# Cache pages of the compressed branch: from two DMA queues to three, with half of them on GpSimd's

## The reference, cut to what matters

```python
past_kc = cc_l[page_table, :, 0].reshape(bs, -1, N_KV, HEAD_DIM)
past_vc = cc_l[page_table, :, 1].reshape(bs, -1, N_KV, HEAD_DIM)
...
def compress(x_raw, pe, w):
    B, Tk = x_raw.shape[:2]
    xb = x_raw.reshape(B, Tk // CMP_BLOCK, CMP_BLOCK, N_KV, HEAD_DIM) + pe[:, None, :]
    return jnp.einsum('bnlgd,lde->bnge', xb, w)
...
    k = rmsnorm(compress(kc_raw, pe[0], w[0]), k_norm_c)
    v = compress(vc_raw, pe[1], w[1])
```

## Time and profile before

| what | us |
|---|---|
| median of 3 runs (4289.74 to 4298.05) | 4290.12 |
| the profiled execution, its own time | 4288.17 |
| its span, from the first to the last instruction | 4286.3 |
| TensorE busy with matmuls, whole span | 3773.1 (88%) |
| VectorE, ScalarE, GpSimd busy, whole span | 1556.0, 941.9, 818.9 |
| first matmul on a cache page to the end of the last | 748.35 to 1081.26 |

### The profile page before, as it was taken

One profiled execution on the slowest core, in us unless ns is written; L12 is line 12 of the kernel. 1 busy time (PEld: TensorE's weight loads), 2 busy tenths in 40 slices (PEclk: granted clock), 3 DMA queues, 4 the chain that ended last, 5 costly groups with the idle time before them and its releaser, 6 DMA issues. The chain is left out here.

```text
span 4286.3 us, 64338 instructions
## 1 busy us (share of the span) xinstructions
PE 3773.1 (88%) x23270; PEld 3191.8 (74%) x23270; DVE 1556.0 (36%) x3867; ACT 941.9 (22%) x2029; POOL 818.9 (19%) x969
## 2 busy tenths in 40 slices
PE   8999997534689999996379999999999999999998
PEld 6888885434466776765368888888888888888887
DVE  4344341010666666552013223432234322432223
ACT  1000000000356666653002111221022100221012
POOL 1010100000254323121002122221222211222112
PEclk9999998777799999997569999999999999999999
DMA  4101005666565443222234555645556555555553
GB/s 166 43 13 55 21 15 172 213 191 196 146 165 139 114 114 102 77 65 77 72 129 142 152 151 169 183 140 151 152 163 179 152 151 152 167 155 152 151 152 109
DMA packets 372823, 558.02 MB, mean 130 GB/s; under 512 B 55655, under 2 KB 155808, under 8 KB 371369
## 3 DMA queue, kind: packets, MB, share of 16 engines
q1 hardware_dynamic: 320984, 502.54, 40.5%
q10 hardware_dynamic: 50697, 43.79, 3.4%
q0 software_dynamic: 864, 7.85, 0.5%
HBM read 480.28 MB, written 78.50 MB: 130 GB/s over the span
## 5 line engine op out<-in xcount | busy, mean ns | idle before, releaser
L319 PE MATMUL ps_z<-x_gained,w_in_sb 128*128 128x257 f32 x2816 | 620.5, 380 | 20.6 <-DVE x_gained L355 20.6
L319 PEld LDWEIGHTS ps_z<-x_gained,w_in_sb 128*128 128x128 f32 x2816 | 533.0, 189 | 102.5 <-issue 21.6
L1746 PE MATMUL ps_tx<-ff,w_ring 128*128 128x257 f32 x1280 | 305.1, 380 | 7.8 <-DVE ff L1894 7.8
L980 ACT ACTIVATE PT_pr<-ps_p 128x384 f32<-128x384 f32 (+4 forms) x576 | 256.6, 496 | 243.6 <-PE ps_p L927 219.5
L1746 PE MATMUL ps_ty<-ff_sums,w_ring 128*128 128x257 f32 x1280 | 305.3, 380 | 0.0
L1746 PE MATMUL ps_ty<-h_sums,w_ring 128*128 128x257 f32 x1280 | 304.2, 379 | 0.2 <-issue 0.2
L1746 PE MATMUL ps_tx<-h_gained,w_ring 128*128 128x257 f32 x1280 | 303.3, 379 | 0.0
L1746 PEld LDWEIGHTS ps_tx<-ff,w_ring 128*128 128x128 f32 x1280 | 242.6, 190 | 44.3 <-issue 8.2
L1746 PEld LDWEIGHTS ps_ty<-ff_sums,w_ring 128*128 128x128 f32 x1280 | 243.1, 190 | 36.8
L1746 PEld LDWEIGHTS ps_ty<-h_sums,w_ring 128*128 128x128 f32 x1280 | 242.2, 189 | 36.7 <-issue 0.6
L1856 POOL TENSOR_TENSOR h<-h,u 128x257 f32<-128x257 f32 x192 | 135.4, 705 | 696.2 <-DVE u L1983 305.8
(11 more groups left out here) (291 smaller groups left out, 5442.4 us busy)
## 6 DMA issues: line engine op xcount, KB each, us to landing
w_ring<-scratch_w_sums SPq DMA_DIRECT2D x640, 256.0 KB, 2.6
w_ring<-in_w_tail SPq DMA_DIRECT2D x480, 256.0 KB, 2.6
w_blocks_pr<-in_w_tail SPq DMA_DIRECT2D x40, 1024.0 KB, 8.2
scratch_w_sums<-w_blocks_pr SPq DMA_DIRECT2D x40, 1024.0 KB, 5.4
pages<-in_cache_cmp SPq DMA_DIRECT2D x256, 128.0 KB, 3.5
pages<-in_cache_cmp ACTq DMA_DIRECT2D x256, 128.0 KB, 3.8
w_in_sb<-in_w_in SPq DMA_DIRECT2D x22, 512.0 KB, 13.8
x_chunk<-in_xT SPq DMA_DIRECT2D x16, 514.0 KB, 6.9
```

The lines of the kernel that those rows point to most:

```text
L319: mm = pe.matmul(o, wg[:, k] if name == "g" else win[:, m, k], aT[:, c % 2, k, h * HF:(h + 1) * HF], start=(k == 0), stop=(k == KT - 1))
L980: act.activation(PT[0:rows, turn_no[x] % 3, g, 0:128 * w], tbank(k, g)[0:rows, 0:w], ACT.Copy).then_inc(s_cp, 1)
L1746: mm = pe.matmul(bank[:, 0:HF], w[:, k], b, start=(name in ("P1", "P6", "P5") and k == 0), stop=(name in ("P2", "P4", "P3") and k == 3), s ...
```

## The change

A buffer's 32 pages are divided into three shares: pages 0 to 7 go to SP, 8 to 15 to ScalarE and 16 to 31 to GpSimd. GpSimd's DMAs count on semaphores of their own, `s_pp`, and TensorE waits for both counts. GpSimd loads its pages of the first turn ahead of the three DMAs of the band, and those of the other seven turns behind them.

```diff
+        s_pp = [ctx.enter_context(nc.semaphore(f"cp_software_pages{b}")) for b in range(2)]
...
-        HALF, AT_ONCE = NPG // 2, 8
+        SHARES = ((0, 8, 8), (8, 8, 8), (16, 16, 8))
...
-                with eng.Fori(0, HALF // AT_ONCE) as j:
-                    base = j * AT_ONCE + HALF * side
+                first, n_pages, at_once = SHARES[side]
+                with eng.Fori(0, n_pages // at_once) as j:
+                    base = j * at_once + first
...
-                                      d["cache_cmp"][ds(page, 1)].rearrange("a p k n -> (a p) k n")).then_inc(s_pg[b], 16)
+                                      d["cache_cmp"][ds(page, 1)].rearrange("a p k n -> (a p) k n")).then_inc((s_pp if side == 2 else s_pg)[b], 16)
...
                 pool.dma_start(cmask[:], d["cmask"]).then_inc(s_cm, 16)
+                pool.wait_ge(s_c, ONE + 16)
+                load_pages(pool, 2, 0)
                 pool.wait_ge(s_line, 3)
...
                 pool.dma_start(t["band"][:], src).then_inc(s_band, 16)
+                with pool.Fori(0, NIT - 1) as i:
+                    load_pages(pool, 2, i + 1)
...
-                        pe.wait_ge(s_pg[b], ONE + 16 * NPG * (i + 1))
+                        pe.wait_ge(s_pg[b], ONE + 16 * 16 * (i + 1))
+                        pe.wait_ge(s_pp[b], 16 * 16 * (i + 1))
```

More of the change, by code:

```diff
@@ L480, in load_pages @@
                 plain(eng)
-                with eng.Fori(0, HALF // AT_ONCE) as j:
-                    base = j * AT_ONCE + HALF * side
+                first, n_pages, at_once = SHARES[side]
+                with eng.Fori(0, n_pages // at_once) as j:
+                    base = j * at_once + first
                     pages = [eng.value_load(ptab[0:1, ds(i * (2 * NPG) + (base + (NPG * b + x)), 1)], min_val=0,
-                                            max_val=d["cache_cmp"].shape[0] - 1) for x in range(AT_ONCE)]
+                                            max_val=d["cache_cmp"].shape[0] - 1) for x in range(at_once)]
                     for x, page in enumerate(pages):
                         eng.dma_start(pg[b][:, ds(base + x, 1)].rearrange("p a k n -> p (a k) n"),
-                                      d["cache_cmp"][ds(page, 1)].rearrange("a p k n -> (a p) k n")).then_inc(s_pg[b], 16)
+                                      d["cache_cmp"][ds(page, 1)].rearrange("a p k n -> (a p) k n")).then_inc((s_pp if side == 2 else s_pg)[b], 16)
         with nc.Block() as block:
```

## The result

| kernel | median us | runs |
|---|---|---|
| before | 4287.31 | 7 (4281.52 to 4298.05) |
| changed | 4305.9 | 7 (4304.03 to 4312.24) |

The ratio is 1.0046 with an interval of 1.0033 to 1.0058: the changed kernel is **slower by about 18.6 us**. The profiled execution of the changed kernel took 4312.24 us (span 4310.5), the highest of its seven, so its 24 us over the profiled execution of before are more than the medians differ by. The prediction was 4223 and faster.

The account below looks back on a forecast made before the run. ScalarE's full instruction stream was taken to bound the 44.5 us turn. Loop 208u - 288.4 plus start debt 48u - 44.2 gave -66.4 us at u = 1.04, so 4223 us, range 4200 to 4355.

Parts of the forecast that it names:

- u: What one page costs GpSimd's stream in the cache loop: 1.04 us, giving a turn of 33.3 us.
- the register steps with the hand-over: In GpSimd's page price: steps around an issue 0.18 us, handing the DMA over some 0.03.
- a quarter of the backlog: Part of GpSimd's issue backlog (2.9 us per eight DMAs) not hidden beside the sequencer: 0.08 us a page.
- rival 1: GpSimd's stream becomes longest: 4350 us if its sequencer stands still per issue, 4480 at 16 ns a row; chance 0.21.
- the formula 256u - 332.6: Whole run's change in us, six and a half loop turns plus the late start: -66.4 at u = 1.04.
- The band's chain: GpSimd's three dependent bias-band DMAs, standing behind its first 32 pages: 33.7 us counted before the second turn's pages.
- the landing L: Time for a buffer's pages to land after issue, before its chunk: taken as 7 us, between 3.6 and 9.2.
- The start debt: Delay of buffer 0's second-turn chunk behind GpSimd's first pages and band: 48u - 44.2, 5.7 us.
- rival 3: In the loop, transfers already bind at 190 GB/s, turn stays 44.5 us: 4294 us, no change; chance 0.04.
- Rival 2: GpSimd's issue backlog isn't queued at all, u = 1.33: 4296 us, no change to slightly slower; chance 0.08.
- Rival 4: GpSimd reads the table faster than ScalarE, u = 0.85, turn of 28 us: about 4176 us; chance 0.06.
- The break-even u = 1.30: GpSimd's page price in us at which the summed change is zero; above it the kernel gets slower.

Follow-up runs that it names:

- experiment 1: Changed kernel with GpSimd reading one table entry and issuing that page's DMA at once, instead of eight reads then eight issues: 4311.56 us.
- experiment 6: Changed kernel with GpSimd's loop written out, without table reads or address registers, loading the same 16 pages of each buffer every turn: 4188.27 us, one run.
- experiment 2: Changed kernel with GpSimd's table reads left out, loading pages 16 to 31 of the pool every turn by the same loop: 4185.22 us.
- experiment 3: Changed kernel with the band's three DMAs put between GpSimd's pages of the first two turns, so it waits for none: 4295.98 us.
- experiment 8: Shares 11, 10, 11 and 11, 11, 10 with the band between, each engine's table reads moved ahead of its buffer wait: 4185.62 and 4179.69 us.
- experiment 5: Changed kernel with each GpSimd page loaded as two DMAs of 64 rows instead of one of 128: 4482.99 us, one run.
- experiment 7: Changed kernel, band's DMAs between pages, SP/ScalarE/GpSimd shares 12, 10, 10; 11, 10, 11; 11, 11, 10: 4211.6, 4208.67, 4214.2 us.

## Why the prediction was wrong

**The step that failed is u, GpSimd's price of a page: 1.04 forecast, 1.42 measured.** The terms, one by one: the read 0.69, measured 0.71; the register steps with the hand-over, 0.18 + 0.03, measured 0.10; the loop 0.06, measured 0.07 (1.42 - 0.71 - 0.64); and the DMA itself, put beside the sequencer but for a quarter of the backlog (0.08), measured 0.53 (experiments 1 and 6). The last term is 0.45 too low, and the register steps, 0.11 too high, hide a part of it. (A quarter of the backlog is 0.09, not 0.08; that slip is worth 2.6 us.) The sequencer stands still for each issue, and a read can't begin until it goes on: the mechanism of rival 1, at a price a little under its 1.54, because the steps around an issue were cheaper.

Two rows had led to it. GpSimd's drain that began at 743.6 beside the band's DMA of 743.58 was read as a sequencer that goes on while an issue is handled. By experiment 1 it goes on when the DMA *begins*; a stand ahead of that left no row there, as GpSimd was waiting anyway. And the three constants stood 0.66 and 0.50 us apart with no register step between them. That spacing, 0.58 on average, is near the 0.53 that issues back to back cost in experiment 6; I took it as a sign of a low price.

**The rest of the sum held, with two errors that cancel in part.** With u = 1.42 the formula 256u - 332.6 gives +31; the last chunk came 18.9 later. By its terms:

- The first 32 pages took 742.71 - 699.4 = 43.3 us for 45.4 by the formula: -2.1.
- The band's chain took 24.3 us (742.71 to 766.99) for 33.7: -9.4. It now ran in a stretch where the DMA engines were busy for 0.85 rather than 1.00, with the first line's DMA 4.2 us on its way in place of 11.0. That the load is why was not tried.
- From the band's issue to buffer 0's chunk 23.9 us for 29.7: -5.8, 4.7 of it the landing L. The page that this chunk waited for landed 2.3 us after its DMA began, and not 7.
- Six turns and a half took 300.7 us for 295.4: +5.3, most of it hold-ups of GpSimd's issues, the longest two 1.00 and 2.84 us:

```profile
877.39 4.36 POOL L488 DMA_DIRECT2D pages<-in_cache_cmp  x7 [1.00 <-issue]
...
937.12 4.42 POOL L488 DMA_DIRECT2D pages<-in_cache_cmp  x7 [2.84 <-issue]
```

VectorE masks the band beside the first; beside the second it has no instruction. What held them was not settled. They are 0.7 us of the 1.5 by which the turn of 47.1 exceeds its stream of 45.6. The rest is the landing of a buffer's last page, 2.3 us at buffer 0's chunk of the second turn and 7.0 at that of the eighth. In the loop itself, then, the forecast's L of 7 was about right.

That is 30.9 - 17.3 + 5.3 = 18.9. The start debt was forecast at 5.7 and measured 790.93 - 784.30 = 6.6: near, but by a longer stream and a shorter chain than I had.

**What was right:** the issue set the turn, not the transfers (rival 3 fell in experiment 2); with ScalarE's load halved its square was no longer waited for; SP and ScalarE were off the path in the changed kernel; the band's chain delayed the second turn (experiment 3). Rival 2 had u at 1.33 and no change or slightly slower, near in its time by luck, as the chain and the landing were priced too high. Its sequencer only waits for its backlog; experiment 1 shows it standing ahead of a DMA even with none. Rival 4 fell on its price for a read: 0.71, no cheaper than ScalarE's 0.69. The break-even u = 1.30 agrees with the sign: 1.42 lies above it.

The Trainium skill, page "DMA: Bandwidth & Descriptors", section "Issuing engines are not separate DMA queues", has the sequencer's time as usually small beside the transfer. Here it is not. On SP or ScalarE a page took 1.28 us of the queue's time before, and its 128 KB take 0.44 us at the 296 GB/s that experiment 8 reached with the same bytes; the two queues before moved 190.

## What to carry to other kernels

When work is to be shared out over queues, price an item on each of them by rows of its own, and where there are none, by the spacing of back-to-back issues: an engine that shows idle may have a sequencer that isn't. Give each queue a share by that price, and not by how free its engine looks; half of the pages on GpSimd lost 0.5%, a quarter won 1.6%, and about a third won 1.7 to 2.6% with the band's DMAs between the pages and, at the best, the reads ahead of the wait. Then look for the ring of a buffer: whatever doesn't need the free buffer, such as reading addresses, belongs ahead of the wait for it.

## What the hardware showed that I had not expected

- GpSimd's sequencer is taken for about 0.53 us by each DMA ahead of its start, for 64 rows as for 128, with an idle engine as with a busy one (experiments 1 and 5; the spacing in 6 agrees). The 16 ns a row that the 16.4 us drain allowed don't exist in these transfers: 128 rows would have taken 2.05 us. The length of a drain is no measure of rows either: in the changed kernel it lasts 9.5 us behind a DMA of 128 rows, as its row on L491 says.

```profile
L491 POOLq DRAIN  x1: 9512/9512/9512, 1089.2 to 1089.2; - x1
```

- How soon a page landed went with what else was on its way, more than with who issued it. In the changed kernel GpSimd's median is 2.6 us for 5.1 and 5.3 of SP's and ScalarE's. But most of GpSimd's DMAs go while the other two queues are quiet. The eight that begin from 807.1 to 811.7, beside pages of both others, take 3.6 to 6.6 us (the first line below), and the last pages of most buffers 5 to 7. With 11, 10 and 11 pages (experiment 7) the order of GpSimd and ScalarE is the other way round:

```profile
DMA to landing us min/median/max: 3.6/6.0/6.6
```

```profile
pages<-in_cache_cmp SPq DMA_DIRECT2D x114, 128.0 KB, 6.4
pages<-in_cache_cmp POOLq DMA_DIRECT2D x110, 128.0 KB, 5.9
pages<-in_cache_cmp ACTq DMA_DIRECT2D x106, 128.0 KB, 4.8
```

- The same reads and issues cost 1.42 us a page in groups of eight and 1.21 in one group of eleven. The register steps beside the reads had a median of 164 ns (113 to 174) in the one and of 113 (46 to 157) in the other.
